# One pair of the last expert's weights in partitions 0 to 63: an fp32 retention, latent-attention and expert trunk on one core

## The chip, the core and the metric

The kernel runs on one core of a Trainium2 chip. The metric is the device time of one execution in microseconds (us), smaller is better. The times shown are of three runs of the kernel before; the profile is that of one more execution.

## What is computed

A trunk of two layers over 272 tokens (16 meta tokens and 256 frames) of width 1024, all in fp32. Each layer mixes tokens (retention and latent attention) and then applies a feed-forward part. In layer 0 that is one dense SwiGLU; in layer 1 it is a routed one, and this change lies wholly in there:

```python
def swiglu(h, w_gate, w_up, w_down):
    return (jax.nn.silu(h @ w_gate) * (h @ w_up)) @ w_down

def moe_swiglu(h, router_w, w_gate, w_up, w_down):
    logits = (h @ router_w).astype(jnp.float32)
    top_val, top_idx = lax.top_k(logits, TOP_K)          # 2 of 8
    ...
    for e in range(N_EXPERTS):
        out = out + gate_dense[..., e:e + 1] * swiglu(h, w_gate[e], w_up[e], w_down[e])
    return out
```

Each expert has three matrices of 1024 x 3584 numbers. The sum of the experts is added to the residual stream, a final RMSNorm follows, and the 256 frames are stored.

## The kernel before

**Stages.** The first layer, the second attention and the routing run up to about 500 us. From there to the end the kernel goes through the eight experts, one pass each. The tokens of an expert are gathered into tiles of 32 slots (`TOK`), three tiles per pass; the last pass has an expert with few tokens and uses only two of the tiles (`LIGHT`, s = 1 and 2).

**The weights.** They come from HBM in *units* of 128 partitions x 3584 numbers (`BIG_UNIT`, 1792 KB). An expert has 24 units: m = 0 to 15 are gate and up weights (four groups g of four units, each unit two 128-row slices k of the contraction over 1024), m = 16 to 23 are down weights (two per group). Two neighbouring units lie side by side in HBM and in SBUF as a *pair* (128 x 7168 numbers, 28,672 B in each partition, 3584 KB).

**The ring.** SBUF holds 12 units (`MOE_SLOTS`), six pairs of buffers `moe_pairs`; the profile calls them all moe_pair. `MOE_PLACES` says which buffer place a unit takes. SyncE (SP) issues every weight transfer in the order of use, on its one queue. Before each it waits until TensorE has released the buffer: the semaphore `w_used` counts the units that TensorE is done with. With `load_two` a whole pair goes as one transfer, once both its buffers are free, which is when the units ten and eleven places back from it have been used. TensorE waits for the semaphore `moe_in` of the pair before its first product.

**The last expert.** `load_last` issues pairs up to m = 19 (`ALONE = 20`), then the four units 20 to 23 one by one, the last in two halves of 896 KB; the second half has the semaphore `last_in`. After its product, tile by tile, the results of the last expert are taken out of PSUM (L1867, L1427), brought back from slots to tokens by 32 products (L1113), added to the residual (L1805), squared, scaled and stored.

**The other way in.** `take_back` on GpSimd (POOL) loads what the other seven experts have summed (`back`, 1024 KB, L642) and the gain of the last norm (`fn_sb`, 512 KB, L640). They go into a ring buffer that no further unit needs, once `w_used` shows that unit 12 of the last expert is done. VectorE adds `back` to the residual (L1826) before it takes out the last expert's results (L1867), in its own order of work.

**TensorE's products.** `up(g)` makes, for each slice k, tile s and quarter q, one product of a 32-column stationary operand (the tokens, `xt`) with 448 moving columns; `down(g)` the same with 256 columns. The four quarters go to four column groups and overlap. Every fp32 product shows as two records in the profile: a pair of up units with two tiles is 64 records, a down unit 56.

Of the kernel before, what the change touches and what calls it, by code (L numbers as in the profile page):

```python
# [41 lines left out]
P = 128  # L42
D = 1024
# [34 lines left out]
ALONE = 20  # L78
# [94 lines left out]
def build(nc, stream, experts, h0, gains, router_w, fnorm, consts, out):  # L173
    with ExitStack() as ctx:
# [112 lines left out]

        moe_slots = [moe_pairs[i // 2][:, i % 2 * BIG_UNIT:(i % 2 + 1) * BIG_UNIT] for i in MOE_PLACES]
        back = moe_slots[0][:, 0:2 * D].rearrange("p (t d) -> p t d", t=2)
        fn_sb, graded = moe_slots[0][:, 2 * D:3 * D], moe_slots[0][:, 3 * D:3 * D + 512]  # L290
        res = moe_slots[1][:, 0:2 * D].rearrange("p (t d) -> p t d", t=2)
        into_tokens = moe_slots[1][:, 2 * D:2 * D + TILES_OF * FRAMES].rearrange("p (s n) -> p s n", s=TILES_OF)
        y_last = moe_slots[1][:, 2 * D + TILES_OF * FRAMES:2 * D + TILES_OF * (FRAMES + 256)].rearrange("p (s n) -> p s n", s=TILES_OF)
# [5 lines left out]
        moe_in, last_in = [sem(f"moe_in{i}") for i in range(MOE_SLOTS)], sem("last_in")  # L299
        direct_used, split_hi, split_lo, w_used = sem("direct_used"), sem("split_hi"), sem("split_lo"), sem("w_used")  # L300
# [106 lines left out]
        def _(sp):  # L407
# [71 lines left out]
            def load_last(it, e):  # L479

                for j in range(ALONE // 2):
                    load_two(it, e, j)
                for m in range(ALONE, EXPERT_UNITS):
                    sp.wait_ge(w_used, it * EXPERT_UNITS + (MOE_SPLIT + m - MOE_SLOTS + 1))
                    if m < EXPERT_UNITS - 1:
                        load_one(e, m)
                    else:
                        load_one(e, m, 0, BIG_UNIT // 2)
                        load_one(e, m, BIG_UNIT // 2, BIG_UNIT, last_in)
# [30 lines left out]
        def _(pool):  # L520
# [116 lines left out]
            def take_back(count):  # L637

                pool.wait_ge(w_used, MOE_SPLIT + EXPERT_UNITS * (count - 1) + MOE_SLOTS + 1)
# [16 lines left out]
        def _(pe):  # L656
# [373 lines left out]
            def expert(it, last=False, tiles=range(TILES_OF), first=False):  # L1030

                def arrival(key):

                    m = MOE_POS[key]
                    alone = (first and m < MOE_SLOTS) or (last and m >= ALONE)
                    if m % 2 == 0:
                        pe.wait_ge(moe_in[m % MOE_SLOTS], it * (16 * EXPERT_UNITS // MOE_SLOTS) + 16 * (m // MOE_SLOTS + 1))
                    elif alone:
                        pe.wait_ge(moe_in[m % MOE_SLOTS], 16 if first else 32)
# [6 lines left out]
                def up(g):  # L1046
# [4 lines left out]
                    for k in range(DK):  # L1051
                        if k % 2 == 0:
                            w = arrival(("w", g, k // 2)).rearrange("p (j q c) -> p j q c", j=2, q=4)
# [947 lines left out]
```

## Time and profile before

| what | value |
|---|---|
| time of three runs | 1356.35 us median (1355.79 to 1358.2) |
| time of the profiled execution | 1355.91 us |
| its span, first to last instruction | 1354.0 us |
| TensorE busy | 1298.6 us, 96% |
| granted TensorE clock, mean | 0.986 of full |
| moved by DMA | 443.89 MB, 328 GB/s over the span |
| of that by SP's queue | 434.14 MB |

The span is the time of the instructions on the core; what lies around it is 1.9 us. TensorE is busy in nearly all slices, but matmuls are pipelined, so that says little; in the expert passes the DMA row shows 9 tenths or more in every slice as well, with 415 to 432 GB/s. A wait of TensorE for a transfer is what tells which of the two leads.

### The profile page before, as it was taken

Reading aid. Unit: us, or ns where it says so; the run is one execution under the profiler, and the core shown is the slowest. Engines: PE = TensorE matmul, PEld = TensorE weight load, DVE = VectorE, ACT = ScalarE, POOL = GpSimd, SP = SyncE. Lnnn points to the kernel's source line nnn. Section 1 sums busy time; section 2 is a strip of 40 time slices with the busy share of each in tenths; the row PEclk is TensorE's granted clock in tenths of the full one; section 3 lists DMA queues with packets and bytes.
Section 4 is the critical chain, followed back from the end, with each engine's and each line's share of the span. In section 5 each row is a group of like instructions: output and inputs, shape, how many; then the busy total and the mean of one; then the engine's idle time right before and its main releaser. Section 6 shows DMA issues by size and latency. Waiting matters only on the chain.

```text
span 1354.0 us, 31059 instructions
## 1 busy us (share of the span) xinstructions
PE 1298.6 (96%) x14058; PEld 938.5 (69%) x14058; DVE 468.8 (35%) x821; ACT 341.2 (25%) x593; POOL 85.0 (6%) x113
## 2 busy tenths in 40 slices
PE   9999999999999999999987879999999999999976
PEld 9889999999998995457652244467676347448534
DVE  7777876777786663110101100100100110110112
ACT  8666443333477643000000000000000000000111
POOL 1000000000000004201011001001001001000100
PEclk9999999999999999999999889999999999999988
DMA  9316545544432389999999999999999999999994
GB/s 373 110 61 250 203 171 187 187 183 161 185 134 92 114 332 429 415 427 422 424 430 418 431 430 416 432 429 418 431 427 423 425 427 431 415 430 427 416 425 172
DMA packets 34207, 443.89 MB, mean 328 GB/s; under 512 B 5600, under 2 KB 7776, under 8 KB 12192
## 3 DMA queue, kind: packets, MB, share of 16 engines
q1 hardware_dynamic: 28368, 434.14, 77.3%
q0 software_dynamic: 5424, 7.51, 2.0%
q8 instruction: 110, 1.80, 0.5%
q10 hardware_dynamic: 288, 0.29, 0.1%
q14 instruction: 17, 0.14, 0.0%
HBM read 438.20 MB, written 5.93 MB: 328 GB/s over the span
## 4 chain that ended last, share of the span: by engine, by line
PE 82%; DMA 13%; DVE 2%; ACT 2%; issue 1%; SPq 0%; ACTq 0%; DVEq 0%
PE bank L668 80%; DMA moe_pair<-experts 13%; DVE w_pairs L1467 1%; DMA ring<-stream 0%; PE bank L672 0%; PE bank L766 0%; DVE nmx L1552 0%; ACT scratch L1224 0%; PE bank L772 0%; ACT w_pairs L1146 0%; ACT scratch L1223 0%; ACT scratch L1221 0%; DVE parts L1481 0%; PE bank L1113 0%; DVE sq L1545 0%
## 5 line engine op out<-in xcount | busy, mean ns | idle before, releaser
L668 PE MATMUL bank<-moe_pair,hT 128*32 128x448 f32 x5376 | 517.0, 545 | 20.8 <-DMA moe_pair<-experts 20.1
L668 PEld LDWEIGHTS bank<-moe_pair,hT 128*32 128x32 f32 x5376 | 243.3, 111 | 289.7 <-issue 216.7
L668 PE MATMUL bank<-parts,w_pairs 128*128 128x272 f32 (+1 forms) x3360 | 427.0, 288 | 1.2 <-DVE w_pairs L1474 0.7
L668 PEld LDWEIGHTS bank<-parts,w_pairs 128*128 128x128 f32 x3360 | 421.6, 188 | 4.6 <-issue 2.5
L668 PE MATMUL bank<-moe_pair,scratch 128*32 128x256 f32 x4704 | 270.5, 388 | 18.6 <-DMA moe_pair<-experts 17.6
L1815 DVE SCALAR_TENSOR_TENSOR hT<-bank,slot_norm,scratch 128x224 f32<-128x224 f32 x96 | 40.6, 423 | 703.3 <-ACT scratch L1376 703.3
L668 PEld LDWEIGHTS bank<-moe_pair,scratch 128*32 128x32 f32 x4704 | 200.1, 112 | 89.7 <-issue 34.1
L1467 DVE TENSOR_TENSOR w_pairs<-ring,w_pairs 128x2048 fp32r<-128x2048 f32 x68 | 154.5, 2287 | 32.2 <-ACT w_pairs L1146 32.1
L1376 ACT ACTIVATE scratch<-bank,norm_now 128x224 f32<-128x224 f32 x96 | 41.2, 447 | 487.5 <-PE bank L668 487.5
L1146 ACT ACTIVATE w_pairs<-ring 128x2048 fp32r<-128x2048 f32 x68 | 129.6, 1912 | 90.1 <-PE bank L668 90.0
L1386 ACT ACTIVATE scratch<-bank,slot_gate 128x256 f32<-128x256 f32 x21 | 9.2, 474 | 246.6 <-PE bank L668 246.6
L1699 DVE TENSOR_TENSOR hT<-hT,bank 128x272 f32<-128x272 f32 x112 | 48.6, 435 | 20.8 <-PE bank L668 19.8
L616 POOL DMA_INDIRECT scratch<-hn_rows,row_of x24 | 24.9, 1039 | 428.5 <-DVE hT L1832 422.7
L625 POOL DMA_INDIRECT acc_rows<-scratch,row_of x21 | 33.4, 1589 | 212.7 <-ACT scratch L1386 208.4
L1818 DVE STREAM_TRANSPOSE scratch<-hT 128x224 f32<-128x224 f32 x96 | 39.5, 412 | 3.3
L668 PE MATMUL bank<-scratch 128*128 128x256 f32 (+4 forms) x144 | 26.6, 353 | 1.3 <-ACT scratch L1239 1.3
L668 PEld LDWEIGHTS bank<-scratch 128*128 128x128 f32 (+1 forms) x144 | 21.8, 181 | 6.6 <-ACT scratch L1289 1.7
L1326 ACT ACTIVATE parts<-scratch 128x544 fp32r<-128x544 f32 x14 | 9.2, 659 | 58.8 <-DVE scratch L1714 58.8
L552 POOL TENSOR_TENSOR scratch<-scratch 128x16 f32<-128x16 f32 x4 | 0.9, 223 | 361.9 <-DVE scratch L1752 361.7
L1201 ACT ACTIVATE scratch<-bank 128x272 f32<-128x272 f32 (+2 forms) x52 | 19.7, 416 | 10.5 <-PE bank L668 9.8
L668 PE MATMUL bank<-scratch,ring 128*128 128x272 f32 (+1 forms) x64 | 15.3, 392 | 1.6 <-ACT scratch L1224 1.6
L668 PEld LDWEIGHTS bank<-scratch,ring 128*128 128x128 f32 x64 | 11.7, 190 | 4.6 <-ACT scratch L1224 2.7
(216 smaller groups left out, 489.6 us busy)
## 6 DMA issues: line engine op xcount, KB each, us to landing
moe_pair<-experts SPq DMA_DIRECT2D x88, 3584.0 KB, 37.2
ring<-stream SPq DMA_DIRECT2D x68, 1024.0 KB, 5.0
moe_pair<-experts SPq DMA_DIRECT2D x15, 1792.0 KB, 15.5
ring<-stream SPq DMA_DIRECT2D x4, 512.0 KB, 7.0
ring<-stream SPq DMA_DIRECT2D x2, 976.0 KB, 4.7
moe_pair<-experts SPq DMA_DIRECT2D x2, 896.0 KB, 47.1
ring<-stream SPq DMA_DIRECT2D x2, 768.0 KB, 10.8
hT<-h SPq DMA_DIRECT2D x4, 272.0 KB, 4.9
```

The costliest lines, as they stand in the source:

```text
L616: pool.indirect_dma_start(out=x_rows[:, s, :], out_offset=None, in_=hn_quarters, in_offset=bass.IndirectOffsetOnAxis(ap=row_of[:, s, n:n + ...
L625: pool.indirect_dma_start(out=acc_quarters, out_offset=bass.IndirectOffsetOnAxis(ap=row_of[:, s, n:n + 1], axis=0), in_=ye[:, s, :], in_of ...
L668: return release(nc.tensor.matmul(dst, lhsT, rhs, start=start, stop=stop), inc, count)
L1146: A(w_hi(n), slot(UNIT_OF[n]), ACT.Copy).then_inc(split_hi, 1)
L1201: A(dst[:, first_of(name, layer):], src(name, rows, cols), ACT.Copy).then_inc(out_free, 1)
L1326: A(ad_hi[c % 2], a_dense, ACT.Copy).then_inc(a_hi_ready, 1)
L1376: A(sil_moe[:, s, :], bank[UP_BANKS[g][s]][:, 0:FQ], ACT.Silu, scale=norm_now[:, s:s + 1]).then_inc(e_silu, 1)
L1386: A(ye[:, s, :], bank[DOWN_BANKS[s]][:, 0:256], ACT.Copy, scale=slot_gate[:, it, s:s + 1]).then_inc(ye_ready, 1)
L1467: V.tensor_tensor(w_lo(n), slot(UNIT_OF[n]), w_hi(n).bitcast(F32), ALU.subtract).then_inc(split_lo, 1)
L1699: V.tensor_tensor(hT[:, d, :], hT[:, d, :], bank[4 + d % 4][:, 0:L], ALU.add).then_inc(h_added, 1)
L1815: V.scalar_tensor_tensor(out=a_moe[:, s, :], in0=bank[UP_BANKS[g][s]][:, FQ:2 * FQ], scalar=slot_norm[:, it, s:s + 1], in1=sil_moe[:, s, : ...
L1818: V.transpose(ht[:, g, s, :], a_moe[:, s, :]).then_inc(ht_ready, 1)
```

## The change

The pair of units 6 and 7 of the last expert (up group 1, slices k = 4 to 7) is called the fold. Its 128 rows no longer go to 128 partitions: rows 0 to 63 go to partitions 0 to 63 of one pair of buffers, rows 64 to 127 to partitions 0 to 63 of the next pair of buffers. Each of these two halves is loaded by eight transfers of eight rows (every fourth partition of a block of 32). The contraction of these slices is then done in two products of 64 rows each, so this pair takes twice as many products. The tokens of rows 64 to 127 are copied to partitions 0 to 63 by ScalarE at the start of the last pass (`xt_up`).

Since the fold takes two pairs of buffers, every later unit moves on by two places (`last_place`), and the wait before its transfer is counted anew (`used_at`). From unit 12 on (`ALONE = 12`) the transfers carry one unit each; two of them are issued behind one wait. `back`, `fn_sb` and the output buffers lie in other buffers of the ring, and `take_back` waits for one unit more.

```diff
@@ -75,7 +75,22 @@
-ALONE = 20
+ALONE = 12
+
+FOLD = 6
+FOLD_K = 2 * (FOLD % (DK // 2))
+
+
+def last_place(m):
+
+    return m + 2 * (m >= FOLD + 2)
+
+
+def used_at(p):
+
+    return p + 1 if p < FOLD + 2 else max(FOLD + 2, p - 1)
+
@@ -285,18 +300,33 @@
+        fold_at = TILES_OF * (DK * TOK + FQ) + 2 * CAP
+        xt_up = h_flat[0:P // 2, fold_at:fold_at + len(LIGHT) * 4 * TOK].rearrange("p (s c) -> p s c", s=len(LIGHT))
+
+
+        def last_view(m):
+
+            half = MOE_PLACES[m % MOE_SLOTS] % 2
+            return moe_pairs[MOE_PLACES[last_place(m) % MOE_SLOTS] // 2][:, half * BIG_UNIT:(half + 1) * BIG_UNIT]
+
+        def fold_view(m, upper):
+
+            half = MOE_PLACES[m % MOE_SLOTS] % 2
+            return moe_pairs[MOE_PLACES[FOLD + 2 * upper] // 2][0:P // 2, half * BIG_UNIT:(half + 1) * BIG_UNIT]
+
-        back = moe_slots[0][:, 0:2 * D].rearrange("p (t d) -> p t d", t=2)
-        fn_sb, graded = moe_slots[0][:, 2 * D:3 * D], moe_slots[0][:, 3 * D:3 * D + 512]
+        back = moe_slots[2][:, 0:2 * D].rearrange("p (t d) -> p t d", t=2)
+        fn_sb, graded = moe_slots[2][:, 2 * D:3 * D], moe_slots[2][:, 3 * D:3 * D + 512]
...
@@ -478,15 +508,39 @@
             def load_last(it, e):
 
-                for j in range(ALONE // 2):
-                    load_two(it, e, j)
+                def free(p):
+
+                    n = p - MOE_SLOTS
+                    sp.wait_ge(w_used, it * EXPERT_UNITS + (MOE_SPLIT + (used_at(n) if n >= 0 else n + 1)))
+
+                def pair(j, p, into):
+
+                    sp.dma_start(moe_pairs[MOE_PLACES[p % MOE_SLOTS] // 2][:, :], experts[e * (EXPERT_UNITS // 2) + j]).then_inc(into, 16)
+
+                for m in range(0, ALONE, 2):
+                    p = last_place(m)
+                    free(p + 1)
+                    if m != FOLD:
+                        pair(m // 2, p, moe_in[p % MOE_SLOTS])
+                        continue
+                    for upper in range(2):
+                        free(p + 2 * upper + 1)
+                        for a in range(0, P // 2, 32):
+                            for b in range(4):
+                                r = slice(a + b, a + 32, 4)
+                                d = slice(a + b + upper * P // 2, a + 32 + upper * P // 2, 4)
+                                sp.dma_start(moe_pairs[MOE_PLACES[p + 2 * upper] // 2][r, :],
+                                             experts[e * (EXPERT_UNITS // 2) + m // 2, d, :]).then_inc(fold_in[upper], 16)
                 for m in range(ALONE, EXPERT_UNITS):
-                    sp.wait_ge(w_used, it * EXPERT_UNITS + (MOE_SPLIT + m - MOE_SLOTS + 1))
...
+                    p, at = last_place(m), BIG_UNIT * (MOE_PLACES[m % MOE_SLOTS] % 2)
+                    if m % 2 == 0:
+                        free(p + 1)
+                    cut = BIG_UNIT // 2 if m == EXPERT_UNITS - 1 else BIG_UNIT
+                    sp.dma_start(last_view(m)[:, 0:cut],
+                                 experts[e * (EXPERT_UNITS // 2) + m // 2, :, at:at + cut]).then_inc(moe_in[p % MOE_SLOTS], 16)
...
@@ -636,7 +690,7 @@
-                pool.wait_ge(w_used, MOE_SPLIT + EXPERT_UNITS * (count - 1) + MOE_SLOTS + 1)
+                pool.wait_ge(w_used, MOE_SPLIT + EXPERT_UNITS * (count - 1) + MOE_SLOTS + 2)
@@ -1062,6 +1128,26 @@
+                def up_folded(g, k, m):
+
+                    for upper in range(2):
+                        if k == FOLD_K:
+                            pe.wait_ge(fold_in[upper], 16 * 8)
+                            if upper:
+                                pe.wait_ge(fold_ready, 1)
+                        w = fold_view(m, upper).rearrange("p (j q c) -> p j q c", j=2, q=4)
+                        for s in tiles:
+                            kk = k - FOLD_K
+                            x = xt_up[:, s - LIGHT[0], kk * TOK:(kk + 1) * TOK] if upper else xt[0:P // 2, s, k * TOK:(k + 1) * TOK]
+                            for q in range(4):
...
+                                mm(bank[UP_BANKS[g][s]][TOK * q:TOK * (q + 1), 0:2 * FQ], x, w[:, k % 2, q, :],
+                                   False, bool(upper) and k == DK - 1, inc, both(s) if inc is e_gu else 1)
@@ -1364,6 +1450,9 @@
+                if final:
+                    act.wait_ge(xg_ready, it * TILES_OF + TILES_OF)
+                    A(xt_up, xt[P // 2:P, LIGHT[0]:TILES_OF, FOLD_K * TOK:(FOLD_K + 4) * TOK], ACT.Copy).then_inc(fold_ready, 1)
```

On SP, in the last pass, these rows stood from the third pair on (moe_pair_53 and the like are the six pairs of buffers; 128x7168 is a pair, 128x3584 a unit):

```order
L465 DMA moe_pair_50<-experts 128x7168
L463 REGISTER_ALU
L465 ISA [waits w_used]
L465 DMA moe_pair_53<-experts 128x7168
L463 REGISTER_ALU
L465 ISA [waits w_used]
L465 DMA moe_pair_51<-experts 128x7168
```

Now there stand at the same place (eight of the eight-row transfers are alike in each of the two groups, here the last two of the first group and the first two of the second, and what follows the second):

```order
L532 DMA moe_pair_53<-experts 8x7168
L514 REGISTER_ALU
L532 ISA [waits w_used]
L532 DMA moe_pair_51<-experts 8x7168
...
L514 REGISTER_ALU
L518 ISA [waits w_used]
L518 DMA moe_pair_52<-experts 128x7168
```

So 16 small transfers stand for one, and a second wait for `w_used` comes before the second eight of them; units 8 and 9, which waited where the second eight now wait, come one wait later. On TensorE, in the last pass, the same pair was:

```order
L668 MATMUL bank<-moe_pair_53,hT 32x448 [waits moe_in6]
L668 MATMUL bank<-moe_pair_53,hT 32x448 x31
L1056 REGISTER_ALU [waits moe_in8]
```

and is now, with one row for each half of a slice:

```order
L722 MATMUL bank<-moe_pair_53,hT 32x448 [waits fold_in0]
L722 MATMUL bank<-moe_pair_53,hT 32x448 x7
L722 MATMUL bank<-moe_pair_51,hT 32x448 [waits fold_ready,fold_in1]
L722 MATMUL bank<-moe_pair_51,hT 32x448 x7
L722 MATMUL bank<-moe_pair_53,hT 32x448 x8
L722 MATMUL bank<-moe_pair_51,hT 32x448 x8
...
L1122 REGISTER_ALU [waits moe_in10]
```

64 products stand where 32 stood, and the next group of products waits for the buffers one pair further on.

## Rows read from the trace of the kernel before

**Rows 1.** The page: engine busy times, clock and DMA in 40 slices.

```profile
PE 1298.6 (96%) x14058; PEld 938.5 (69%) x14058; DVE 468.8 (35%) x821; ACT 341.2 (25%) x593; POOL 85.0 (6%) x113
PEclk9999999999999999999999889999999999999988
GB/s 373 110 61 250 203 171 187 187 183 161 185 134 92 114 332 429 415 427 422 424 430 418 431 430 416 432 429 418 431 427 423 425 427 431 415 430 427 416 425 172
```

**Rows 2.** The chain that ended last, from 1200 us on: start, us, what.

```profile
1277.62 44.43 DMA moe_pair<-experts
1322.05 0.14 issue
1322.19 19.62 PE bank L668 x328
1341.81 0.02 issue
1341.84 0.43 DVE moe_pair L1867
```

**Rows 3.** Timeline of TensorE, last pass: start, us, what, idle time before it.

```profile
1253.16 30.30 PE L668 MATMUL bank<-moe_pair,hT 128*32 128x448 f32 x319
1285.19 6.22 PE L668 MATMUL bank<-moe_pair,hT 128*32 128x448 f32 x64 [1.73 <-DMA moe_pair<-experts]
1293.75 6.22 PE L668 MATMUL bank<-moe_pair,hT 128*32 128x448 f32 x64 [2.34 <-DMA moe_pair<-experts]
1302.35 7.74 PE L668 MATMUL bank<-moe_pair,hT 128*32 128x448 f32 x64 [2.38 <-DMA moe_pair<-experts]
1312.24 7.94 PE L668 MATMUL bank<-moe_pair,scratch 128*32 128x256 f32 x112 [2.15 <-DMA moe_pair<-experts]
1322.19 20.02 PE L668 MATMUL bank<-moe_pair,scratch 128*32 128x256 f32 x336 [2.01 <-DMA moe_pair<-experts]
```

**Rows 4.** Windows: us, PE, PEld, DVE, ACT, POOL busy (x), PEclk, DMA share, GB/s.

```profile
1150.00:1200.00 50.00, 50.00 (x536) 22.72 (x532) 7.06 (x18) 4.03 (x9) 0.00 (x0) 1.00 1.01 423
1300.00:1310.00 10.00, 7.65 (x64) 2.18 (x64) 0.03 (x1) 0.51 (x2) 0.00 (x0) 0.83 0.99 422
...
1320.00:1324.00 4.00, 1.99 (x25) 1.20 (x25) 0.00 (x0) 0.00 (x0) 0.00 (x0) 0.82 0.92 381
1324.00:1326.00 2.00, 2.00 (x24) 1.32 (x20) 0.00 (x0) 0.00 (x0) 0.00 (x0) 0.51 0.77 325
1326.00:1328.00 2.00, 2.00 (x41) 1.45 (x37) 1.40 (x1) 0.00 (x0) 0.00 (x0) 1.00 0.56 237
1328.00:1330.00 2.00, 2.00 (x44) 1.48 (x40) 0.90 (x1) 0.00 (x0) 0.00 (x0) 1.00 0.50 215
1330.00:1332.00 2.00, 2.00 (x44) 1.47 (x40) 0.00 (x0) 0.00 (x0) 0.00 (x0) 1.00 0.52 222
1332.00:1334.00 2.00, 2.00 (x44) 1.43 (x39) 0.00 (x0) 0.00 (x0) 0.00 (x0) 1.00 0.46 184
1334.00:1336.00 2.00, 2.00 (x45) 1.42 (x39) 0.00 (x0) 0.00 (x0) 0.00 (x0) 1.00 0.51 211
1336.00:1338.00 2.00, 2.00 (x44) 1.48 (x40) 0.00 (x0) 0.00 (x0) 0.00 (x0) 1.00 0.47 191
1338.00:1340.00 2.00, 2.00 (x44) 1.48 (x40) 0.00 (x0) 0.00 (x0) 0.00 (x0) 1.00 0.13 54
```

**Rows 5.** SP's queue by line from 1150 us (L465 pairs, L458 single units), issue to landing.

```profile
L465 SPq DMA_DIRECT2D moe_pair<-experts x16: 332/333/346, 1153.2 to 1277.6; - x16
DMA to landing us min/median/max: 31.5/33.6/44.4
...
L458 SPq DMA_DIRECT2D moe_pair<-experts x5: 333/333/333, 1280.6 to 1292.1; - x5
DMA to landing us min/median/max: 46.3/47.8/47.9
```

**Rows 6.** Products of 32 rows against products of 128 rows (tile moe_pair, from 1200 us).

```profile
L668 PE MATMUL bank<-moe_pair,scratch x1120: 376/379/634, 1215.9 to 1341.8; 128*32 128x256 f32 x187
L1113 PE MATMUL bank<-moe_pair x32: 374/374/478, 1342.4 to 1344.1; 32*128 32x256 f32 x32
```

**Rows 7.** The page: DMA queues (packets, MB, share of 16 engines over the span).

```profile
q1 hardware_dynamic: 28368, 434.14, 77.3%
q0 software_dynamic: 5424, 7.51, 2.0%
q8 instruction: 110, 1.80, 0.5%
```

**Rows 8.** Timelines of POOL and DVE, and DMA issues from 1200 us.

```profile
1297.30 0.62 POOL L640 DMA_DIRECT2D moe_pair<-fnorm  x1 [37.99 <-PE bank L668]
1326.60 2.29 DVE L1826 TENSOR_TENSOR trig<-trig,moe_pair 128x2048 f32<-128x2048 f32 x1 [12.66 <-DMA moe_pair<-acc_rows]
1341.84 0.42 DVE L1867 COPY moe_pair<-bank 128x256 f32<-128x256 f32 x1 [12.94 <-PE bank L668]
...
moe_pair<-acc_rows POOLq DMA_DIRECT2D x1, 1024.0 KB, 28.7
out<-moe_pair SPq DMA_DIRECT2D x1, 256.0 KB, 2.5
```

More of the change, by code:

```diff
@@ L299, in build @@
         moe_in, last_in = [sem(f"moe_in{i}") for i in range(MOE_SLOTS)], sem("last_in")
+        fold_in, fold_ready = [sem(f"fold_in{i}") for i in range(2)], sem("fold_ready")
         direct_used, split_hi, split_lo, w_used = sem("direct_used"), sem("split_hi"), sem("split_lo"), sem("w_used")
@@ new lines, in load_last @@
+                for m in range(ALONE, EXPERT_UNITS):
+                    p, at = last_place(m), BIG_UNIT * (MOE_PLACES[m % MOE_SLOTS] % 2)
[4 more added lines that the diff above has]
+                                 experts[e * (EXPERT_UNITS // 2) + m // 2, :, at:at + cut]).then_inc(moe_in[p % MOE_SLOTS], 16)
+                    if cut < BIG_UNIT:
+                        sp.dma_start(last_view(m)[:, cut:BIG_UNIT],
+                                     experts[e * (EXPERT_UNITS // 2) + m // 2, :, at + cut:at + BIG_UNIT]).then_inc(last_in, 16)
@@ L1034, in arrival @@
                     m = MOE_POS[key]
-                    alone = (first and m < MOE_SLOTS) or (last and m >= ALONE)
+                    if last:
+                        p = last_place(m)
+                        if m % 2 == 0:
+                            laps = p // MOE_SLOTS + 1 - (p >= MOE_SLOTS and p % MOE_SLOTS in (FOLD, FOLD + 2))
+                            pe.wait_ge(moe_in[p % MOE_SLOTS], it * (16 * EXPERT_UNITS // MOE_SLOTS) + 16 * laps)
+                        elif m >= ALONE:
+                            pe.wait_ge(moe_in[p % MOE_SLOTS], 32)
+                        return last_view(m)
+                    alone = first and m < MOE_SLOTS
                     if m % 2 == 0:
@@ L1038, in arrival @@
                     elif alone:
-                        pe.wait_ge(moe_in[m % MOE_SLOTS], 16 if first else 32)
+                        pe.wait_ge(moe_in[m % MOE_SLOTS], 16)
                     return moe_slots[m % MOE_SLOTS]
@@ L1051, in up @@
                     for k in range(DK):
+                        m = MOE_POS["w", g, k // 2]
+                        if last and m in (FOLD, FOLD + 1):
+                            up_folded(g, k, m)
+                            continue
                         if k % 2 == 0:
@@ L1064, in up @@
                                    w[:, k % 2, q, :], k == 0, k == DK - 1, inc, both(s) if inc is e_gu else 1)
+                def up_folded(g, k, m):
[9 more added lines that the diff above has]
+                            for q in range(4):
+                                inc = None
+                                if upper and q == 3 and s == TILES_OF - 1:
+                                    inc = w_used if k % 2 else None
+                                elif upper and q == 3 and k == DK - 1:
+                                    inc = e_gu
+                                mm(bank[UP_BANKS[g][s]][TOK * q:TOK * (q + 1), 0:2 * FQ], x, w[:, k % 2, q, :],
+                                   False, bool(upper) and k == DK - 1, inc, both(s) if inc is e_gu else 1)
                 def down(g, final=False):
```

11 lines of the change are left out of this document (3 added, 8 removed).

## The prediction, made before the changed kernel was run

> **What bounds the kernel now.** I read the page first. TensorE is 96% busy, and from the sixteenth slice on the GB/s row stands at 415 to 432 [rows 1]: two candidates. The chain that ended last decides between them at the end: a transfer of expert weights lands at 1322.05, then 19.62 us of products run without a gap, then the take-out begins at 1341.84 [rows 2]. TensorE's timeline of the last pass shows the same earlier: five pairs in one run of 30.30 us, then a wait for a transfer before each of the next five blocks, 1.73, 2.34, 2.38, 2.15 and 2.01 us, 10.6 us in sum [rows 3]. In the last pass, with two tiles for three, TensorE is faster than the transfers (6.22 us of products per pair; the blocks start 8.6 to 10.0 us apart), so the transfers lead.
>
> Then I cut the end into small windows and read the DMA share [rows 4]. It is 1.01 and 0.99 as long as all 16 engines work, falls between 1320 and 1326, and stays at 0.46 to 0.52 (184 to 222 GB/s, against 422) until 1338. So at the end eight of the 16 engines work and eight are done. What the share exceeds 0.5 by after 1320 is 0.42 x 4 + 0.27 x 2 + 0.06 x 2 = 2.34 us, so the early eight stop on average at 1320 + 2.34/0.5 = 1324.7, the last of them near 1327.5, where the share reaches 0.50. The late eight: (0.50 + 0.52 + 0.46 + 0.51 + 0.47 + 0.13) x 2 / 0.5 = 10.4 us after 1328, so 1338.4 on average, and the last at 1340.0 (issue at 1292.1 plus 47.9 [rows 5]). The two halves lie 13 us apart, though each transfer of 128 partitions loads them alike. TensorE can use a unit only when the late half has landed. One thing that could load only some engines is the instruction queue: 0.5% of 16 engines over 1354 us is 108 engine-us, or 13.5 us on each of eight [rows 7]. That fits the gap; that it lies on those eight is my inference.
>
> **The change part by part.**
>
> *The fold's transfers.* Rows 64 to 127 of a pair are 64 x 28,672 B = 1.84 MB. At the rate of one half, 215 GB/s [rows 4], that is 8.5 us. If the late half is the one that serves partitions 64 to 127, and eight rows in partitions 0 to 63 stay on the other, the late half ends 8.5 us sooner (1340.0 to 1331.5) and the early half 8.5 us later (1327.5 to 1336.0). The last landing is then at 1336.0: 4.0 us earlier. The gap of 13 us would ask for 6.5, so the move overshoots, and the early half becomes the last.
>
> *Sixteen small transfers for one.* No such transfer is in the trace. Nearest are the single and half units at the end: four or five boundaries between 1328 and 1338, where the five windows average 205 GB/s, against 212 for half of 423. That is 3% of 10 us, 0.3 us, or at most 0.1 us a boundary. Times 16: at most 1.6 us; below, nothing. The far bound is a store alone, 2.5 us from issue to landing [rows 8], 40 us if nothing overlapped, which the full share before 1320 speaks against: transfers queue up there and none shows such a hole. I take 0.3 us. On SP each issue costs 0.33 us plus some 0.2 around it [rows 5], 16 of them 8.5 us, in two groups; SP's pairs go out (1277.6 - 1153.2)/15 = 8.3 us apart on average, so a group of eight, 4.2 us, is hidden between two releases. Without that cover the next pair would be issued up to 4 us late.
>
> *The ring is one pair shorter.* Each transfer behind the fold waits for a release one pair later. For the early half this costs nothing, as it also has 8.5 us more to do in between. The late half loses one pair of lead (9 us) and has 8.5 us less to do. It was issued 31.5 us or more ahead of its landing [rows 5], of which 8.5 is its own transfer: 23 - 9 - 10 leaves some 3 to 5 us at units 8 and 9, above a start of about 2. A hole of 2 us there would put the late half at 1333.5, still before 1336.0.
>
> *Products of 64 rows.* Products of 32 rows take 374 ns, those of 128 rows 379, at the same 256 columns [rows 6]. So I give 64 rows the full price: 64 records more at 30.30/319 = 0.095 us, +6.1 us. The zero end is excluded by the same rows. TensorE's last pass is then, without waits, nine times 6.06 = 54.5 us of up units and eight down units. A down unit at full clock: 336 records in 20.02 us include about 3.4 us at half clock, so (20.02 - 1.7)/336 = 0.0545 us a record, 3.1 us a unit, 24.4 in sum. 1253.2 + 54.5 + 24.4 = 1332.1, against a last landing at 1336.0. The 10.6 us of waits cover the 6.1; if they didn't, the whole 6.1 would come on top.
>
> *Single units from 12 on.* They let TensorE start a pair half a pair earlier. Behind the last landing this changes nothing (the last unit was halved already). A unit lands each 4.3 us and takes 3.1, so TensorE keeps up, and after the last half unit 28 records, 1.5 us, are left. Before, the take-out began 1.8 us after the last landing; I keep 1.8.
>
> *Clock.* The granted clock is 0.83 for 1300 to 1310 and 0.51 for 1324 to 1326, right behind waits [rows 4], the lower level (1.2 GHz) for about 3.4 us at a time; such a stretch costs 1.7 us. Now TensorE waits less until about 1320 and again 1 to 3 us before units 20, 21 and 22. A low stretch in the last 6 us would cost up to 1.7 us. I take 0.4.
>
> *`back` and the copy.* POOL issued at 1297.3, behind unit 12. Now it waits for unit 13, which ends at 1253.2 + 8 x 6.06 = 1301.7, so 4.6 us later. `back` was in at 1326.6 and its sum took 2.29 [rows 8]; 4.6 later that is 1333.5, still before the take-out at 1337.8. The copy on ScalarE (a copy of 128 x 256 takes VectorE 0.42 us there) comes before work that waits for products anyway.
>
> Sum: -4.0 + 0.3 + 0.4 = -3.3 us; the chain behind 1341.84 stays 12.2 us. From the profiled execution's own 1355.91 us this gives 1352.6. That execution is 0.44 us under the median of the three; I leave the forecast at 1352.6 us.
>
> **A rule against it.** The late engines are eight by the share of 0.5 [rows 4]. The Trainium skill ("DMA: Bandwidth & Descriptors", Latency and other measured facts) says that engines 7 and 15 are usually slower than the others; two late engines would show a share of 0.13, so the trace disagrees with it here. By that rule the fold would only load a late engine more, and its end would be 8.5 us later. The same page (Rules for kernel authors) advises against transfers to disjoint partition halves, since both use all 16 engines; by it the last landing stays at 1340.0. Its section on why a DMA increments its semaphore by 16 says that eight rows take only eight engines, and that these are the lowest-numbered; no row here can show that.
>
> **The rivals.**
>
> *It doesn't move the load.* Eight-row transfers are spread over both halves, or cost as much as they save (0.25 us each, 16 x 0.25 = 4). The last landing stays near 1340.0 and the time at 1355.5 to 1356.5. For it: no row has such a transfer. Against: 0.1 us at most per boundary. Chance 0.17.
>
> *The late half is the one that gets the fold.* The profile names no engine, so which partitions are late is open. Then 1340.0 + 8.5, take-out at 1350.3, time 1364.4: slower. It decides from the first microsecond, since every one added to the late half is one of time. A lesser form: a price per small transfer over 0.25 us, at 0.5 us each 1360. Against the first form the rows say nothing; I give 0.14 together, on a judgement only that the inference on the instruction queue has a fixed side.
>
> *TensorE becomes the bound.* Several low-clock stretches (three before, 5.1 us) put its 1332.1 to 1337.2, and the take-out to 1339.5: 1353.6 to 1354.5. Chance 0.12. If both terms I added are nothing: 1351.9.
>
> **How the numbers follow.** A measurement of this kernel tells about 0.2% from no change, 2.7 us. The forecast holds 0.57 (1351.3 to 1353.6). With a part of the TensorE rival that is still over 2.7 us faster I say faster 0.64; same: the first rival and the rest of the third, 0.22; slower 0.14. The range must leave out no more than 0.2: from 1351.0 to 1357.0, which drops the slow rival (0.14) and little below.
>
> **What would show it.** Windows after 1320: the share should stay near 1 until about 1325, and fall to 0 by 1336 with the last stretch at 0.5 short. TensorE's timeline: no wait before the block that waited 1.73, 2.34, 2.38 and 2.15, and small ones from 1320 on; the fold as 128 records in 12.1 us. The SP rows: 16 issues of L532 with landings under 30 us. The prediction is wrong if the share stays at 0.5 for longer than 13 us at the end (wrong half), if it has holes around 1245 to 1262 (price of small transfers), or if DVE's wait for `back` ends after 1337.

## The result, and the profile after

| | before | changed |
|---|---|---|
| median of four runs | 1356.58 us (1355.79 to 1358.2) | 1363.62 us (1363.0 to 1367.21) |
| ratio | | 1.006, 95% interval 1.0048 to 1.0071 |
| profiled execution, its span | 1355.91, 1354.0 us | 1367.21, 1365.4 us |
| TensorE busy, granted clock | 1298.6 us, 0.986 | 1307.6 us, 0.980 |

The changed kernel is slower by 7.0 us; 1352.6 was forecast, with a range up to 1357.0. The profiled execution was the slowest of the four, 3.6 us over their median.

The page of the changed kernel, engine busy times and the GB/s row, answers to [rows 1]:

```profile
PE 1307.6 (96%) x14122; PEld 884.1 (65%) x14122; DVE 469.0 (34%) x821; ACT 341.8 (25%) x594; POOL 83.4 (6%) x113
GB/s 367 111 62 247 208 165 183 186 185 176 166 134 109 91 370 428 417 427 418 428 429 421 432 429 421 430 426 420 432 426 418 429 430 420 425 428 405 377 404 127
```

The row follows that of before up to the 36th slice; then 405, 377, 404 and 127 stand for 427, 416, 425 and 172. The loss lies in the last pass.

The chain that ended last in the changed kernel (start, us, what), beside [rows 2]:

```profile
1275.81 35.43 PE bank L722 x240
...
1311.42 34.27 DMA moe_pair<-experts
1345.69 0.04 issue
1345.73 7.41 PE bank L722 x104
1353.17 0.43 DVE moe_pair L1956
```

The take-out begins at 1353.17 instead of 1341.84, 11.3 us later, and that is the whole difference of the two profiled times (1367.21 - 1355.91). Before, the last wait for a transfer was at 1322; now it is at 1345.7, so the transfers set the end.

TensorE's timeline of the last pass (start, us, what, idle time ahead), beside [rows 3]:

```profile
1250.36 19.88 PE L722 MATMUL bank<-moe_pair,hT 128*32 128x448 f32 x208
1275.81 47.41 PE L722 MATMUL bank<-moe_pair,hT 64*32 64x448 f32 x368 [5.56 <-DMA moe_pair<-experts]
1323.04 15.28 PE L722 MATMUL bank<-moe_pair,scratch 128*32 128x256 f32 x276
1339.78 3.65 PE L722 MATMUL bank<-moe_pair,scratch 128*32 128x256 f32 x60 [1.46 <-DMA moe_pair<-experts]
1345.73 7.79 PE L722 MATMUL bank<-moe_pair,scratch 128*32 128x256 f32 x112 [2.31 <-DMA moe_pair<-experts]
```

The five waits of before are gone, as forecast. In their place stands one of 5.56 us in the middle of the fold, a gapless block that is longer by far, and two waits near the end.

Windows of the changed kernel (us, then busy time and count of PE, PEld, DVE, ACT and POOL, clock, DMA share, GB/s), beside [rows 4]:

```profile
1262.00:1270.00 8.00, 8.00 (x88) 2.84 (x80) 2.35 (x6) 1.10 (x3) 0.00 (x0) 1.00 1.03 413
1276.00:1290.00 14.00, 14.00 (x77) 3.49 (x74) 0.00 (x0) 0.00 (x0) 0.00 (x0) 0.50 0.99 420
1290.00:1294.00 4.00, 4.00 (x28) 1.16 (x24) 0.00 (x0) 0.00 (x0) 0.00 (x0) 0.50 0.65 276
1294.00:1297.00 3.00, 3.00 (x20) 0.52 (x16) 0.89 (x3) 0.78 (x2) 0.00 (x0) 0.50 0.38 162
...
1336.00:1338.00 2.00, 2.00 (x40) 1.06 (x32) 0.00 (x0) 0.00 (x0) 0.00 (x0) 1.00 0.90 378
1338.00:1340.00 2.00, 0.54 (x8) 0.16 (x8) 1.83 (x1) 0.00 (x0) 0.00 (x0) 1.00 0.16 68
1340.00:1342.00 2.00, 2.00 (x44) 1.21 (x40) 0.46 (x1) 0.00 (x0) 0.00 (x0) 1.00 0.13 57
1342.00:1344.00 2.00, 1.43 (x24) 0.58 (x16) 0.00 (x0) 0.00 (x0) 0.00 (x0) 1.00 0.12 48
1344.00:1346.00 2.00, 0.27 (x4) 0.20 (x8) 0.00 (x0) 0.00 (x0) 0.00 (x0) 0.87 0.12 43
1346.00:1348.00 2.00, 2.00 (x24) 0.92 (x20) 0.00 (x0) 0.00 (x0) 0.00 (x0) 0.50 0.09 36
```

This is the view that tells most. Before, the tail stood at 0.5 for 10 us: eight engines of 16. Now the share falls from 0.90 to 0.16 within 4 us and then stands at 0.12 to 0.13 until 1346, and 0.125 is 2 engines of 16. So the share at the end is no longer that of a half; two engines alone have work left.

SP's rows of the changed kernel (issue duration min/median/max in ns, from when to when; then issue to landing), beside [rows 5]; L532 is the fold, L542 the last half unit:

```profile
L532 SPq DMA_DIRECT2D moe_pair<-experts x16: 644/644/1067, 1232.7 to 1248.0; - x16
...
L542 SPq DMA_DIRECT2D moe_pair<-experts x1: 333/333/333, 1312.9 to 1312.9; - x1
DMA to landing us min/median/max: 37.0/37.0/37.0
```

An issue of eight rows takes SP 0.64 us instead of 0.33. The last half unit, issued at 1312.9, landed at 1349.9; before, the last landing was at 1340.0.

### The profile page after: what moved, and what is told of

Read it like the earlier page. It is cut to its first block, busy times and chain, and to the rows that moved or that the text cites. A ratio compares the mean times of both kernels' runs of the same rounds, so it can differ in the third digit from the quotient of the medians.

```text
span 1365.4 us, 31246 instructions
## 1 busy us (share of the span) xinstructions
PE 1307.6 (96%) x14122; PEld 884.1 (65%) x14122; DVE 469.0 (34%) x821; ACT 341.8 (25%) x594; POOL 83.4 (6%) x113
## 4 chain that ended last, share of the span: by engine, by line
PE 80%; DMA 15%; DVE 2%; ACT 2%; issue 1%; SPq 1%; ACTq 0%; DVEq 0%
PE bank L722 78%; DMA moe_pair<-experts 14%; DVE w_pairs L1556 1%; DMA ring<-stream 1%; PE bank L726 0%; PE bank L820 0%; SPq L532 0%; DVE nmx L1641 0%; ACT scratch L1310 0%; PE bank L826 0%; ACT w_pairs L1232 0%; ACT scratch L1309 0%; ACT scratch L1307 0%; DVE parts L1570 0%; PE bank L1199 0%
## 5 line engine op out<-in xcount | busy, mean ns | idle before, releaser
L722 PE MATMUL bank<-moe_pair,hT 128*32 128x448 f32 (+1 forms) x5440 | 532.0, 554 | 25.4 <-DMA moe_pair<-experts 24.6
L722 PEld LDWEIGHTS bank<-moe_pair,hT 128*32 128x32 f32 (+1 forms) x5440 | 208.0, 112 | 345.5 <-issue 313.4
L722 PE MATMUL bank<-moe_pair,scratch 128*32 128x256 f32 x4704 | 261.8, 384 | 15.8 <-DMA moe_pair<-experts 15.0
L722 PEld LDWEIGHTS bank<-moe_pair,scratch 128*32 128x32 f32 x4704 | 180.2, 112 | 98.5 <-issue 22.6
L1556 DVE TENSOR_TENSOR w_pairs<-ring,w_pairs 128x2048 fp32r<-128x2048 f32 x68 | 154.6, 2288 | 32.2 <-ACT w_pairs L1232 32.1
```

The costliest lines, as they stand in the source:

```text
L722: return release(nc.tensor.matmul(dst, lhsT, rhs, start=start, stop=stop), inc, count)
L1556: V.tensor_tensor(w_lo(n), slot(UNIT_OF[n]), w_hi(n).bitcast(F32), ALU.subtract).then_inc(split_lo, 1)
```

## The experiments

From the rows above I formed this theory, **L**: the engines that carry eight-row transfers are a fixed eight, and two of them belong to the eight that are late. The fold puts eight more packets of 28,672 B on each of the eight; at 1.06 us each, as the trace's packet records have it, that is 8.5 us more on the two late ones, and 8.5 us less on the six others that are late. The rivals are a price of the small transfers themselves (**S**), and the 64-row products, which ran at clock 0.50 for 21 us (**T**). I made three groups of runs; the kernels of one group share their runs of before.

**First group: which engines, told by how the pair is spread.** Runs of before: median 1355.83 us. In `spread`, the changed kernel loads each half of the fold by one 64-row transfer:

```diff
-                        for a in range(0, P // 2, 32):
-                            for b in range(4):
-                                r = slice(a + b, a + 32, 4)
-                                d = slice(a + b + upper * P // 2, a + 32 + upper * P // 2, 4)
...
+                        r, d = slice(0, P // 2), slice(upper * P // 2, (upper + 1) * P // 2)
...
-                            pe.wait_ge(fold_in[upper], 16 * 8)
+                            pe.wait_ge(fold_in[upper], 16)
```

> The changed kernel, but each half of the fold comes by one transfer of 64 rows in place of eight of eight rows. Theory L (some of the eight engines that eight-row transfers use are late ones, and the fold put 8.5 us more on them): a transfer of 64 rows loads all engines alike, so the last landing is back near 1341 and the time near 1357, within 2 us of before. Theory T (the products of 64 rows, which ran at half clock and took 21.3 us, are what costs): the products are the same, so the time stays near 1363. Theory S (small transfers cost by themselves): near 1357 as well.

The other three are the kernel before, with units 6 and 7 in their own 128 partitions and in products of 128 rows, but loaded by smaller transfers:

```diff
+ROWS_OF = [slice(h + a + b, h + a + 32, 4) for h in (0, 64) for a in (0, 32) for b in range(4)]            # in8
+ROWS_OF = [slice(64, 128)] + [slice(b, b + 51, 10) for b in range(10)] + [slice(60, 64)]                   # in6mix
+ROWS_OF = [slice(64, 128)] + [slice(a + b, a + b + 16, 4) for a in (0, 16, 32, 48) for b in range(4)]      # in4mix
...
+                    for r in ROWS_OF:
+                        sp.dma_start(moe_pairs[MOE_PLACES[SPLIT_AT] // 2][r, :], experts[e * (EXPERT_UNITS // 2) + j, r, :]).then_inc(fold_in, 16)
```

> The kernel before, with only the transfer of the pair of units 6 and 7 of the last expert cut into 16 transfers of eight rows, each to its ordinary partitions. Products, ring and waits are those of before. Theory L, if the engine goes by the row's place in the transfer: the same eight engines carry all of it, last landing 8.5 us later, time 1365. If the engine goes by the destination's partition: load as before, 1356.6. Theory T: 1356.6, as no product has changed. Theory S: the fold's 16 transfers cost what they cost in the changed kernel, 1363.

> The kernel before; of the pair of units 6 and 7 of the last expert, rows 64 to 127 by one transfer, rows 0 to 59 by ten transfers of six rows and rows 60 to 63 by one of four, all to their ordinary partitions. Theory L, if the late ones among the first eight engines are the last two: six early engines carry 14.7 rows for 8 and end at 1334.6, all others 4 for 8 and end at 1335.8; time 1352.4. If a late engine is among the first six: its end is 7 us later than before, time 1363.5. Theory S: at least as slow as before.

> As the one before, but rows 0 to 63 by sixteen transfers of four rows. Theory L, if the first four engines are early ones: they carry 20 rows for 8, 12.7 us more, and end at 1340.2, the others at 1335.8; time 1356.8, about as before. If a late engine is among the first four: last landing at 1352.7, time 1369. Theory S: 16 small transfers, slower than before by 4 us or more.

| kernel | median us | ratio to before, 95% interval |
|---|---|---|
| spread | 1376.34 | 1.0153 (1.0136 to 1.0170) |
| in8 | 1382.36 | 1.0191 (1.0174 to 1.0208) |
| in6mix | 1384.82 | 1.0212 (1.0195 to 1.0229) |
| in4mix | 1376.11 | 1.0148 (1.0131 to 1.0165) |

All four are 20 to 29 us slower than before, more than any theory gave. Where the time goes shows in windows of spread (its middle, and one near its end) and of in8:

```profile
1246.00:1256.00 10.00, 7.84 (x133) 5.28 (x129) 0.00 (x0) 1.58 (x5) 0.31 (x1) 0.95 1.02 211
...
1352.00:1354.00 2.00, 2.00 (x44) 1.23 (x40) 1.91 (x1) 0.00 (x0) 0.00 (x0) 1.00 0.50 211
```

```profile
1248.00:1270.00 22.00, 20.22 (x231) 7.83 (x220) 2.35 (x6) 2.73 (x8) 4.77 (x3) 1.00 1.03 251
```

In their middle the share is 1.02 and 1.03 but the rate 211 and 251 GB/s: the engines are all occupied and carry half to six tenths of the usual 423. The median packet of 28,672 B takes 2.22 us in that window of spread and 2.04 in that of in8, against 1.06 usually. The changed kernel has no such stretch. Here is the window in which its fold is under way:

```profile
1244.00:1262.00 18.00, 18.00 (x248) 9.26 (x243) 0.00 (x0) 2.05 (x7) 4.77 (x3) 1.00 0.96 390
```

The kernel before had 424 GB/s at 1.01 in the same window. So the times of this group can't be set against L's numbers: they hold a price that the change does not pay.

The ends of the traces can be read all the same, since only the last engines count there. Windows at the end of in6mix, then of in4mix:

```profile
1360.00:1366.00 6.00, 5.28 (x95) 3.14 (x95) 0.00 (x0) 0.00 (x0) 0.00 (x0) 1.00 0.06 25
```

```profile
1356.00:1358.00 2.00, 1.30 (x24) 0.62 (x20) 0.00 (x0) 0.00 (x0) 0.00 (x0) 1.00 0.28 118
1358.00:1360.00 2.00, 2.00 (x44) 1.44 (x39) 0.00 (x0) 0.00 (x0) 0.00 (x0) 1.00 0.19 73
1360.00:1362.00 2.00, 2.00 (x44) 1.48 (x37) 0.00 (x0) 0.00 (x0) 0.00 (x0) 1.00 0.03 14
```

With six-row transfers one engine is alone at the end (1/16 is 0.0625), for the whole 6 us shown; with eight-row transfers in place (in8) the share is 0.10 to 0.16 from 1354 to 1364, about two engines; with four-row transfers the share tapers off, and there is no stretch in which one or two engines stand alone. In spread, which loads all 16 alike, the end stands at 0.50 again: the eight of before. This is as L has it if one late engine is among the first six and another is the seventh or eighth, and none among the first four. The Trainium skill ("DMA: Bandwidth & Descriptors", the section on why a DMA increments its semaphore by 16) says that such transfers use the lowest-numbered engines, as many as the rows give; the tails of 0.13, 0.06 and none agree with the number, and the trace does not say whether they are the lowest-numbered.

**Second group: load alone, and the products alone.** Runs of before: median 1356.44 us. `extra8`, `extra6` and `extra4` are the kernel before with eight copies from HBM to HBM on SP's queue, of 8, 6 or 4 rows of 28,672 B, ahead of the last pass's fourth pair:

```diff
+                    if j == 3:
+                        for i in range(8):
+                            sp.dma_start(sink[8 * i:8 * (i + 1), :], experts[e * (EXPERT_UNITS // 2), 8 * i:8 * (i + 1), :]).then_inc(sink_in, 16)
```

> The kernel before, with eight transfers more on SP's queue ahead of the last expert's fourth pair: each copies eight rows of 28,672 B from HBM to an unused buffer in HBM, so no partition of SBUF is touched. If a transfer of eight rows uses the first eight engines, each of them gets 8 packets of 1.06 us more, 8.5 us. Theory L (two of these eight are late ones): the last landing moves from 1340.0 to 1348.5 and the time by about 8.5 us, to 1364.5; at the end two engines alone work for some 8 us (share 0.13). If all eight were early ones they would end at 1336 and the time would stay at 1356.

> As extra8, with eight transfers of six rows: the first six engines get 8.5 us more each. From the run with rows by six, where one engine alone landed last, theory L expects one late engine among the first six: time again near 1364.5, with a share of one engine (0.06) at the end. If the two late ones are the seventh and the eighth: 1356.

> As extra8, with eight transfers of four rows: only the first four engines get 8.5 us more each. Theory L with the late ones behind the fourth: no engine passes 1340 (the four end near 1336), time 1356 to 1357. If a late one is among the first four: 1364.5. Any price of small transfers as such would show here as in extra8.

`pe64` is the kernel before, whose products of units 6 and 7 are each done twice over rows 0 to 63; rows 64 to 127 of these units are left out (but for the first product, once more over 128 rows):

```diff
...
+                                    mm(bank[UP_BANKS[g][s]][TOK * q:TOK * (q + 1), 0:2 * FQ], xt[0:64, s, k * TOK:(k + 1) * TOK],
+                                       w[0:64, k % 2, q, :], False, False)
+                                    mm(bank[UP_BANKS[g][s]][TOK * q:TOK * (q + 1), 0:2 * FQ], xt[0:64, s, k * TOK:(k + 1) * TOK],
+                                       w[0:64, k % 2, q, :], False, k == DK - 1, inc, both(s) if inc is e_gu else 1)
...
```

> The kernel before with its transfers as they are; only the products of units 6 and 7 of the last expert are changed: each is done twice, over rows 0 to 63 alone (rows 64 to 127 are left out, so this computes something else). Theory T (products of 64 rows hold the clock low and cost the 7 us): this block takes near 21 us at half clock, and the time is 1362 or more. Theory L: TensorE has 10 us of waits to cover it, and the time stays within 2 us of before. If the low clock in the changed kernel came only from its wait of 5.6 us ahead of the block, there is no such wait here and the block takes 12.1 us at full clock.

| kernel | median us | ratio to before, 95% interval | over before |
|---|---|---|---|
| extra8 | 1360.75 | 1.0030 (1.0019 to 1.0042) | +4.3 us |
| extra6 | 1359.79 | 1.0026 (1.0016 to 1.0035) | +3.4 us |
| extra4 | 1358.55 | 1.0016 (1.0006 to 1.0026) | +2.1 us |
| pe64 | 1356.89 | 1.0004 (0.9995 to 1.0014) | +0.5 us |

The copies did not do what I made them for. The queue's count of packets, reads and writes, rose from 28368 to 28624 in extra8: 128 reads and 128 writes for eight copies, 16 packets of 14,336 B in each and not eight of 28,672. The trace has them on all 16 engines, and so for 6 and 4 rows (10,752 and 7,168 B). They do not tell one engine from another. They do calibrate: a packet of 14,336 B takes 0.535 us, eight are 4.3, and 4.3 were measured; for 6 and 4 rows eight packets are 3.2 and 2.2 us, and 3.4 and 2.1 were measured. Here a microsecond of work added to every engine in the last pass cost one microsecond, and eight small transfers cost nothing above their bytes.

pe64 rules out the doubled products at full clock. Its last pass on TensorE:

```profile
1250.84 43.35 PE L668 MATMUL bank<-moe_pair,hT 128*32 128x448 f32 x450
...
1323.45 20.02 PE L668 MATMUL bank<-moe_pair,scratch 128*32 128x256 f32 x336 [2.02 <-DMA moe_pair<-experts]
```

With 66 records more it runs for 43.35 us in one block, 96 ns a record (95 in [rows 3]), and the time is that of before within the interval. The doubling costs what the prediction gave it, and the waits cover it. In pe64 the clock stayed at 1.00, though, so this run says nothing of the 21 us at 0.50 that the changed kernel has; those are taken up below.

**Third group: load on eight engines, with no fold at all.** Runs of before: median 1356.59 us. `store8` is the kernel before with 27 stores from eight partitions to HBM, 8,192 B in each, nine behind each of the last pass's first three pairs; `store4` has four partitions:

```diff
+                    if j < 3:
+                        for i in range(9):
+                            sp.dma_start(sink[9 * j + i], trig[0:32:4, 0:2 * D]).then_inc(sink_in, 16)
```

> The kernel before, with 27 small stores more on SP's queue, nine behind each of the first three pairs of the last expert: eight partitions of SBUF (0, 4, ... 28) of 8192 B each to an unused buffer in HBM. The copies inside HBM (extra8, extra6, extra4) were cut over all 16 engines; with one side in eight partitions a transfer should stay on eight engines, the same eight as the fold's. Each gets 27 packets of some 0.31 us, 8.4 us. Theory L: two of them are late ones, last landing near 1348.4, time near 1364.5, and at the end a share of two engines (0.13) for some 8 us. If the eight are all early: 1356.5. Theory S (small transfers or SP's time as such): the same loss in store4.

> As store8, with four partitions (0, 4, 8, 12) per store, so the first four engines alone. The tail of the run with rows by four showed no engine standing alone. Theory L: none of the first four is a late one, they end near 1336, the last landing stays at 1340 and the time within 2 us of before. Theory S: as store8.

`rows8` is the changed kernel with eight neighbouring rows in each transfer, `singles` the kernel before with single units from 12 on:

```diff
-                            for b in range(4):
-                                r = slice(a + b, a + 32, 4)
-                                d = slice(a + b + upper * P // 2, a + 32 + upper * P // 2, 4)
+                            for b in range(0, 32, 8):
+                                r = slice(a + b, a + b + 8)
+                                d = slice(a + b + upper * P // 2, a + b + 8 + upper * P // 2)
```

```diff
-ALONE = 20
+ALONE = 12
...
-                    sp.wait_ge(w_used, it * EXPERT_UNITS + (MOE_SPLIT + m - MOE_SLOTS + 1))
+                    if m % 2 == 0:
+                        sp.wait_ge(w_used, it * EXPERT_UNITS + (MOE_SPLIT + m - MOE_SLOTS + 2))
```

> The changed kernel, but each of the 16 transfers takes eight neighbouring rows (0 to 7, 8 to 15, ...) in place of every fourth. Engine by place in the transfer: the same eight engines, but now two to four of them write to the partitions of one group at a time. In the runs with rows by six and by four and in spread, the queue carried 211 to 251 GB/s at a share of 1.0 where that was so, so the fold would be slower: near 1376. If only the number and size of transfers counted: 1363, as the changed kernel.

> The kernel before, with only the single units from 12 on in place of from 20 on (two units behind one wait, as in the changed kernel). All theories: the last landing is not touched; TensorE starts some pairs earlier, which the last landing takes back: within 1 us of before.

| kernel | median us | ratio to before, 95% interval | over before |
|---|---|---|---|
| store8 | 1363.53 | 1.0050 (1.0033 to 1.0067) | +6.9 us |
| store4 | 1356.42 | 0.9996 (0.9987 to 1.0006) | -0.2 us |
| rows8 | 1388.69 | 1.0229 (1.0212 to 1.0246) | +32.1 us |
| singles | 1356.40 | 0.9996 (0.9987 to 1.0006) | -0.2 us |

Windows of store8, then of store4:

```profile
1330.00:1336.00 6.00, 6.00 (x89) 4.00 (x82) 2.29 (x1) 0.00 (x0) 0.00 (x0) 0.74 0.73 309
1336.00:1338.00 2.00, 2.00 (x44) 1.48 (x40) 0.00 (x0) 0.00 (x0) 0.00 (x0) 1.00 0.52 212
...
1340.00:1342.00 2.00, 2.00 (x44) 1.42 (x37) 0.00 (x0) 0.00 (x0) 0.00 (x0) 1.00 0.14 57
1342.00:1346.00 4.00, 4.00 (x80) 2.95 (x76) 0.00 (x0) 0.00 (x0) 0.00 (x0) 1.00 0.13 52
1346.00:1350.00 4.00, 3.80 (x72) 2.59 (x67) 0.42 (x1) 0.38 (x1) 0.00 (x0) 1.00 0.01 4
```

```profile
1336.00:1338.00 2.00, 1.29 (x26) 0.97 (x28) 0.00 (x0) 0.00 (x0) 0.00 (x0) 1.00 0.46 190
1338.00:1340.00 2.00, 2.00 (x44) 1.44 (x37) 0.00 (x0) 0.00 (x0) 0.00 (x0) 1.00 0.23 91
1340.00:1342.00 2.00, 2.00 (x44) 1.50 (x40) 0.00 (x0) 0.00 (x0) 0.00 (x0) 1.00 0.01 4
```

27 packets of 8,192 B are 221 KB on each of eight engines, 8.2 us at 27 KB a microsecond (28,672 B in 1.06 us). Without a fold, without 64-row products and without a change of the ring, this gives +6.9 us, where the change gave +7.0, and the same tail of two engines from 1340 on. The same number of transfers on four engines costs nothing and its tail ends within 1 us of before. That decides for L, and against a price of the transfers' number: store4 issues as many.

The traces hold one more record that shows the engines one by one, though without their numbers. The stores left 216 packets of 8,192 B in store8 and 108 in store4, so eight and four to a transfer. A weight transfer has 16 parts, and the semaphore rises by one as each part lands. For the last half unit these 16 times are, in us:

| kernel | parts land at |
|---|---|
| before | eight at 1321.9 to 1327.4, eight at 1337.6 to 1340.1 |
| changed | fourteen at 1337.8 to 1339.2, two at 1347.5 and 1349.8 |
| store8 | two at 1322.9 and 1327.6, six at 1330.9 to 1336.0, six at 1338.3 to 1340.8, two at 1346.1 and 1347.1 |
| store4 | four at 1321.9 to 1327.5, four at 1333.2 to 1335.6, eight at 1337.5 to 1340.9 |

That is L part by part. In store8 two early engines and six late ones end as before, six early ones and two late ones some 8 us later; in store4 the four that are loaded are all early, and still end before the late ones. It also tells why 8.2 us gave only 6.9: less 8.2, the two loaded late parts would land at 1337.9 and 1338.9, inside the late group but ahead of its last one (1340.1 before).

In rows8, TensorE waited 12.71 us for the fold's second half, and the low rate of the first group is back:

```profile
1250.00:1270.00 20.00, 13.28 (x136) 4.98 (x132) 2.35 (x6) 2.20 (x7) 4.77 (x3) 0.95 1.01 238
...
1301.69 46.87 PE L722 MATMUL bank<-moe_pair,hT 64*32 64x448 f32 x368 [12.71 <-DMA moe_pair<-experts]
```

With every fourth partition of 32 in a transfer the rate is 390 GB/s (the window of 1244 to 1262 above), with eight neighbours 238, for the same bytes in the same partitions. singles shows that the finer units near the end cost nothing and bring nothing.

## Why the prediction was wrong

**The step that failed** is the first of the change's parts: "If the late half is the one that serves partitions 64 to 127, and eight rows in partitions 0 to 63 stay on the other". The share of 0.5 told me how many engines are late, eight, and I made them a half of the partitions. They are not: two of the late eight are among the eight that the fold loads (tail 0.13, and the landings of store8), and so six are among the others. With late engines on both sides, load that is moved from one side to the other lengthens the tail by what it adds. The term of -4.0 us for the last landing is +9.9 in the profiled execution, 1349.9 against 1340.0. By packets it is +8.5. The rest lies in one packet: from 1343.53 to 1344.50 one of the two late engines moved 16,384 B for the instruction queue, and its next packet of 7,168 B took 0.75 us instead of 0.27, 1.4 to 1.5 us together. Its part of unit 21 landed at 1339.7 and that of unit 22 at 1345.7, 6.0 us apart, where the other late engine took 4.2.

**The rival that came nearest** was "the late half is the one that gets the fold", 1364.4 us, 0.8 over the median measured, within a chance of 0.14. Its last landing of 1348.5 is 1.4 us ahead of the measured one. Its size is right because one late engine is enough; its picture of eight late engines under the fold is wrong. The weak point was the weighing: I had one inference, on the instruction queue, and no row that named a side, and still gave the good side 0.57.

**The rule against it** deserved more. The share of 0.5 speaks against only two late engines before the change, and it was right to say so. But I dropped with the number what the rule said of the change, a fold that loads a late engine, 8.5 us more. Only the second part needs to be true, and it needs one engine.

**Small transfers.** 0.3 us were given, in a range of 0 to 1.6. The runs show no part of the loss as theirs: store4 with 27 issues is as fast as before, and the changed kernel's last landing is accounted for without them. A dip there is, 0.96 and 390 GB/s while the fold is under way against 1.01 and 424 before, but not on the late engines that set the end: theirs was work without a hole, as the next paragraph shows. The issue on SP is dearer than forecast (0.64 us, one each 0.84 us or so within a group, against 0.33 and 0.53), which did no harm.

**The fold's landing.** No wait was forecast ahead of it, and there was one of 5.56 us, until 1275.76. Two of its eight engines were late already and each had 16 packets of the pair where eight others had none. The landings show it: of the first half's 64 parts, 48 (six engines) had landed by 1255.2 and the last 16 came from 1258.0 to 1267.2, of the second half's the last 16 from 1267.6 to 1275.8, one each 0.6 us or so, which is two engines at work. Behind that wait the products of 64 rows ran at clock 0.50, the lower level (1.2 GHz), from 1276 to 1297, where I had said that TensorE would wait less until about 1320 and had taken 0.4 us for low stretches; the fold took some 21 us instead of 12.1. Released late by this, unit 16 was issued only at 1297.14 and unit 17 behind it, and the share sank to 0.65 and 0.38 ahead of them, where I had it near 1 until about 1325. Most engines ran dry, the two late ones did not: their parts of unit 15 landed at 1309.2 and 1309.9 and those of unit 16 at 1313.5 and 1314.2, 4.3 us later, which is one unit's work (eight packets of 14,336 B at 0.535 us). That is why the hole isn't in the time: store8 has no such hole (a share of 0.99 to 1.02 from 1266 to 1320), and the same loss. For the same reason the ring's step, "one pair shorter", held where it counted, though the 10 in its sum of 23 - 9 - 10 has no row behind it.

**Products of 64 rows** at full price: right (pe64, 96 ns against 95). **Single units**: right (singles). **`back`**: right in kind; it was in at 1338.17, where 1331 was worked out, and its sum ended at 1340.5, before the take-out. The prediction had named 1337 as a sign of being wrong; it came true and cost nothing. **Behind the last landing** 1.8 us were kept; it was 3.3 (1353.17 - 1349.9). The last wait was for unit 22, until 1345.69, and the products of units 22 and 23 then took 7.4 us without a gap, with the clock at 0.50 from 1346 to 1348. That is the 1.4 us by which the take-out moved more than the landing.

**What is not settled.** The profiled execution has a take-out 11.3 us later, the medians differ by 7.0, and the other executions have no trace that would say which microseconds they saved. Which transfers make eight engines late in the first place, two here and six there, was not tried. In the trace of before the mean landing of the late eight parts lies 0.5 us behind that of the early eight at 489 us, 3.8 at 727, 7.8 at 948, 11.5 at 1187 and 13.6 at the end, so the gap grows through the expert passes. The instruction queue's packets since 489 us are 83 us in sum, 10.4 on each of eight engines if they lie on the late ones: most of a growth of 13.1 but not all of it (the 13.5 of the prediction counts packets from before the gap opened). One such packet is seen on a late engine, the one at 1343.53; for the others it stays an inference. Whether a fold that loads only the first four engines, where none is late, would gain was not run: in4mix can't tell, as it pays the price of the low rate (+20.3 us in all).

## What to carry to other kernels

A DMA share of 0.5 tells how many engines are late, not which. Before load is moved off the late ones, load a few engines with plain stores of the same bytes and look at the tail: the number of engines left alone is read off as share times 16, and one run each of eight and four would have settled this case ahead of all the work on the ring. And a transfer to part of the partitions is not only a question of how many engines it takes: read GB/s beside the share, since a share of 1.0 at 211 GB/s is half the usual rate, which the share alone hides.

## What the runs showed of the hardware that was not expected

- **The rate depends on which rows go together.** Into partitions 0 to 63, eight rows four apart ran at 390 GB/s at share 0.96; eight neighbouring rows at 238 at 1.01, one 64-row transfer for each half at 211 at 1.02. Transfers of eight rows four apart into all 128 partitions (in8) had 251 at 1.03. What makes the slow forms slow is not shown: no run was made to tell their causes apart.
- **A copy from HBM to HBM of eight, six or four rows is cut over all 16 engines**, unlike one into SBUF or out of it: packets of 14,336, 10,752 and 7,168 B for rows of 28,672, and 128 landings for eight copies.
- **How long the clock stays low behind a wait differs.** Behind the wait of 5.56 us, 64-row products stayed at 0.50 for all of their 21 us, and in spread for as long (below). Products of 128 rows behind a wait of 25.75 us in in8 took 14.61 us for 128 records, 12.2 at full clock, so some 5 us were at the low level. Products of 64 rows with no wait ahead (pe64) kept the full one. Rows of spread, of in8's timeline, and of pe64:

```profile
1288.00:1309.00 21.00, 21.00 (x114) 5.15 (x115) 0.77 (x2) 0.79 (x2) 0.00 (x0) 0.50 0.94 396
```

```profile
1294.36 14.61 PE L676 MATMUL bank<-moe_pair,hT 128*32 128x448 f32 x128 [25.75 <-DMA moe_pair<-experts]
```

```profile
1268.00:1284.00 16.00, 16.00 (x166) 6.39 (x162) 2.35 (x6) 1.24 (x3) 0.00 (x0) 1.00 1.02 422
```
